# Edge tiles of a dilated attention: two chunks of 128 keys instead of one of 64 and one of 128

## The reference, cut to what matters

```
def dilated_group(q, k, v, dilation, half_steps, bias):
    L = s // dilation                     # tokens of one residue class
    out, lse = banded_attention(to_sub(q), to_sub(k), to_sub(v), half_steps, half_steps, bias, None)

# banded_attention
offs = arange(3 * block)[None, :] - block - arange(block)[:, None]
mask = (abs(offs) <= half_window) & kvalid
logits = where(mask, q @ k * scale + bias, NEG_INF)
e = exp(logits - m);  ssum = sum(e);  out = (e / ssum) @ v
```

## Time and profile before

| | |
|---|---|
| time, median of 3 runs | 2906.52 us (2903.6 to 2906.72) |
| the profiled execution's own time | 2898.05 us |
| its span | 2895.9 us |
| PE busy | 2720.7 us (94%) |
| DVE, ACT, POOL busy | 1310.1 (45%), 1022.5 (35%), 724.5 (25%) us |
| TensorE clock granted, mean | 0.98 |
| branch C in the two layers | from about 707 to 995 us and from 2139 to 2427 us |

### The profile page before, as it was taken

How to read it: one execution, slowest core, us unless ns; L and a number is a source line. 1 busy time by engine, 2 the same in 40 slices (tenths; PEclk the granted TensorE clock), 3 DMA queues, 4 the chain that set the end, 5 groups by cost and what they waited for, 6 DMA issues and landing times.

```text
span 2895.9 us, 36963 instructions
## 1 busy us (share of the span) xinstructions
PE 2720.7 (94%) x13836; PEld 2240.9 (77%) x13836; DVE 1310.1 (45%) x2815; ACT 1022.5 (35%) x2085; POOL 724.5 (25%) x449
## 2 busy tenths in 40 slices
PE   7899999999999989999879999998999999899996
PEld 6677887878888768877776777787888887688875
DVE  3575366522434355523145734585234444455222
ACT  4464116412444425511135631173024443354012
POOL 2100331033434232222220014301333333222231
PEclk9999999999999999999989999999999999999998
DMA  7000210021111221112050011100212113111122
GB/s 241 27 1 10 55 43 19 1 59 45 47 44 41 75 72 30 37 46 95 23 183 15 1 28 46 42 10 10 64 40 52 40 40 103 37 37 37 44 95 80
DMA packets 204194, 146.00 MB, mean 50 GB/s; under 512 B 21688, under 2 KB 187192, under 8 KB 203976
## 3 DMA queue, kind: packets, MB, share of 16 engines
q1 hardware_dynamic: 190188, 137.08, 16.7%
q10 hardware_dynamic: 13824, 6.49, 0.8%
HBM read 124.44 MB, written 27.49 MB: 52 GB/s over the span
## 4 chain that ended last, share of the span: by engine, by line
PE 83%; DVE 9%; ACT 3%; issue 2%; DMA 1%; POOL 1%; SPq 1%; ACTq 0%; POOLq 0%; DVEq 0%; another core or an unknown queue 0%
PE ps L892 21%; PE ps L855 9%; PE ps L856 9%; PE ps L857 9%; PE ps L998 5%; PE ps L1023 4%; PE ps L955 4%; PE ps L956 4%; PE ps L957 4%; PE ps L1071 3%; PE ps L1039 3%; PE ps L1008 2%; DVE pt_slots L1814 2%; PE ps L1000 1%; DVE nm L1650 1%
## 5 line engine op out<-in xcount | busy, mean ns | idle before, releaser
L2051 POOL CAST wh<-wraw 128x1024 fp32r<-128x1024 f32 (+2 forms) x162 | 176.2, 1088 | 2058.8 <-PE ps L857 873.1
L855 PE MATMUL ps<-xh,wh 128*128 128x512 f32 x1120 | 442.1, 395 | 3.0 <-ACT pt_split L1542 2.2
L856 PE MATMUL ps<-xl,wh 128*128 128x512 f32 x1120 | 438.2, 391 | 0.0
L857 PE MATMUL ps<-xh,wl 128*128 128x512 f32 x1120 | 438.1, 391 | 0.0
L2053 POOL TENSOR_TENSOR wl<-wraw,wh 128x1024 fp32r<-128x1024 f32 (+2 forms) x162 | 421.0, 2599 | 13.0
L892 PE MATMUL ps<-xh,wh 128*128 128x512 f32 x864 | 353.9, 410 | 3.1 <-ACT att L1368 1.2
L892 PE MATMUL ps<-xh,wl 128*128 128x512 f32 x864 | 344.4, 399 | 0.0
L892 PE MATMUL ps<-xl,wh 128*128 128x512 f32 x864 | 344.2, 398 | 0.0
L855 PEld LDWEIGHTS ps<-xh,wh 128*128 128x128 f32 x1120 | 212.3, 190 | 47.5 <-ACT pt_split L1542 3.0
L857 PEld LDWEIGHTS ps<-xh,wl 128*128 128x128 f32 x1120 | 211.7, 189 | 44.7
L856 PEld LDWEIGHTS ps<-xl,wh 128*128 128x128 f32 x1120 | 212.1, 189 | 43.2
(11 more groups left out here) (213 smaller groups left out, 4748.1 us busy)
## 6 DMA issues: line engine op xcount, KB each, us to landing
wraw<-in_w_in_dram SPq DMA_DIRECT2D x128, 512.0 KB, 3.9
xres<-acc SPq DMA_DIRECT2D x2, 4096.0 KB, 15.8
toep<-toep_row SPq DMA_DIRECT2D x32, 256.0 KB, 10.7
wraw<-in_w_branch_dram SPq DMA_DIRECT2D x64, 128.0 KB, 3.9
wraw<-in_w_out_dram SPq DMA_DIRECT2D x16, 512.0 KB, 3.7
acc<-xres SPq DMA_DIRECT2D x16, 512.0 KB, 7.7
dil_out<-cst ACTq DMA_DIRECT2D x96, 66.0 KB, 1.6
att<-dil_out SPq DMA_DIRECT2D x48, 132.0 KB, 2.5
```

The costliest lines, as they stand in the source:

```text
L855: pe.matmul(dst, ah, bh, start=i == 0, stop=False)
L856: pe.matmul(dst, ah, bl, start=False, stop=False)
L857: last = pe.matmul(dst, al, bh, start=False, stop=i == len(ks) - 1)
L2051: inc(pool.tensor_copy(high, raw), w_hi)
```

## The change

- The windows of values all have 128 rows. For group 0 they are the seven of the middle and those at 0, 128, 768 and 896 (eleven in all, three groups of transposes of 4, 4 and 3). For group 1 they are those at 0 and 128 of each of the four classes (eight, two groups of 4).
- An edge unit has two chunks of 128 like any other. The first tile of a class takes keys 0 to 255, the last one the last 256; of these the unit sees 192. The probabilities are written at an offset `p0` in `prob`, which is 0 or 64, so that each key stands in its chunk's place; the 64 keys it does not see keep probabilities of zero.
- The zeros are written by a `memset` of 128x64 on DVE ahead of the unit's `maxima`: in group 0 for all four edge units of a pass, in group 1 for the first four units of the first pass only, since later units use the same slot of `prob` with the same part unseen. That is 12 in a layer and 24 in the launch.
- An edge unit's probabilities then come out of PSUM in one copy of 128x256, since both chunks have the same height.
- `at`, where the keys of the logits' product begin, is now the class's own 256 keys for the last tile of a class in group 1. The size of that product, 256 columns, is as before.

```diff
@@ windows and chunks
-                            windows = [(c, P * j - 64, P) for c in range(r) for j in range(1, nq)]
-                            windows += [(c, 0, 64) for c in range(r)] + [(c, L - 64, 64) for c in range(r)]
+                            windows = [(c, P * j - 64, P) for c in range(r) for j in range(1, nq)] if nq > 2 else []
+                            windows += [(c, k0, P) for c in range(r) for k0 in sorted({0, P, L - 2 * P, L - P})]
...
-                                    chunks, at = [], lo
-                                    while at < hi:
-                                        m = 64 if at == 0 or at == L - 64 else P
-                                        chunks.append((m, at - lo, cv[hp][0:m, place[(c, at)], cols]))
-                                        at += m
-                                at = min(k0, S - 2 * P)
+                                    first = min(lo, L - 2 * P)
+                                    at, p0 = c * L + first, lo - first
+                                    chunks = [(P, x, cv[hp][:, place[(c, first + x)], cols]) for x in (0, P)]
+                                    if nk < 2 * P and (nq > 2 or hp == 0 and c == 0):
+                                        fresh = slice(0, p0) if p0 else slice(nk, 2 * P)
@@ exps (ACT)
-                    dst = u["prob"][:, 0:u["nk"]]
+                    p0 = u.get("p0", 0)
+                    dst = u["prob"][:, p0:p0 + u["nk"]]
@@ maxima (DVE)
-                    nk = u["nk"]
-                    ins = dve.tensor_tensor_reduce(u["prob"][:, 0:nk], u["logits"][:, 0:nk], u["bias"], 1.0, 3.0e38,
+                    nk, p0 = u["nk"], u.get("p0", 0)
+                    if u.get("fresh"):
+                        dve.memset(u["prob"][:, u["fresh"]], 0.0)
+                    ins = dve.tensor_tensor_reduce(u["prob"][:, p0:p0 + nk], u["logits"][:, 0:nk], u["bias"], 1.0, 3.0e38,
                                                    ALU.add, ALU.min, mx[:, s % U_MAX:s % U_MAX + 1] if u.get("sink") else dst)
```

More of the change, by code:

```diff
@@ L484, in build @@
                                 cols = slice(e * HD, (e + 1) * HD)
+                                fresh = None
                                 if L == P:
                                     k0, nk, b0 = i * P, P, 0
+                                    at, p0 = min(k0, S - 2 * P), 0
                                     chunks = [(P, 0, cv[hp][:, i, cols])]
@@ L491, in build @@
                                     k0, nk, b0 = c * L + lo, hi - lo, lo - (j * P - 64)
-                                    chunks, at = [], lo
-                                    while at < hi:
-                                        m = 64 if at == 0 or at == L - 64 else P
-                                        chunks.append((m, at - lo, cv[hp][0:m, place[(c, at)], cols]))
-                                        at += m
-                                at = min(k0, S - 2 * P)
+                                    first = min(lo, L - 2 * P)
[3 more added lines that the diff above has]
+                                        fresh = slice(0, p0) if p0 else slice(nk, 2 * P)
                                 unit(cq_stack[hp][:, e, i * P:(i + 1) * P], ck_stack[hp][e][:, 0, at:at + 2 * P],
                                      table_g[:, hp * 2 + e, b0:b0 + nk], chunks, "act",
-                                     st=i, head=hp * 2 + e, e=e, g=g, hp=hp, seen=(k0 - at, nk),
+                                     st=i, head=hp * 2 + e, e=e, g=g, hp=hp, seen=(k0 - at, nk), p0=p0, fresh=fresh,
                                      k_rest=ck_stack[hp][e][:, 1, at:at + 2 * P])
```

## The result

| | before | after |
|---|---|---|
| median of the first runs | 2905.06 us (2901.41 to 2906.72, 4 runs) | 2872.6 us (2869.93 to 2878.59, 4 runs) |
| profiled execution, span | 2895.9 us | 2876.5 us |
| mean granted clock, profiled execution | 0.980 | 0.977 |

The ratio is 0.9893 (0.9873 to 0.9912), 31 us; the two medians are 32.5 us apart. The spans of the two profiled executions are only 19.4 us apart.

What follows compares the result with a forecast made beforehand. PE's own list was taken to bound branch C. 10.8 + 0.3 - 0.2 - 0.6 = 10.3 us a layer, 20.6 in two, off the median 2906.5 gave 2886 us; own spread 2881 to 2891, 8-in-10 range 2878 to 2897.

Steps and rivals of the forecast that it cites:

- PE's own list sets the pace, and the height of 64 rows is what costs: Branch C: PE time saved shortens the kernel; edge units' `values` take 0.62 to 0.64 us against 0.39 because of height.
- The rival that something else in an edge unit costs: Edge units in branch C: the 0.25 us belongs to something that stays; 2906 us, no change, 4% chance.
- 0.278 us for a unit in steady running: Group 1's steady steps: extra cost of an edge unit, 22 units a layer, 6.1 us won.
- 0.26 us for each of the other 18 units of a layer and 0.3 us for the value transposes: Edge units in group 0 or at pass ends: 4.7 us a layer won; value transposes: net 0.3 us a layer.
- Memsets, 0.2 us a layer: DVE in branch C: 4 of 24 memsets exposed, 0.1 us each, costing 0.2 us a layer.
- Given back at the fills, 0.6 us a layer: Group 1's passes: a PE wait at a fill behind DVE's stack work, 2 x 0.3 us a layer lost.
- Sum in branch C: Branch C ends 10.3 us sooner in each layer, 20.6 us in two.
- the change is taken from that median: 2886 us: Whole kernel: the gain is subtracted from the runs' median, 2906.5 us, giving 2886 us, 0.7% faster.
- Slower: Rival at the edge units: wider pieces cost PE weight loads, with all memsets exposed; 8.3 us, 2915 us, 3% chance.
- DVE as pacer: Rival in group 1's passes: DVE's stack work takes back 8 to 16 us, about half the gain; 2896 us, 10% chance.

Runs made afterwards that it cites:

- h64_first: Changed kernel, but the second chunk's value matmul reads 64 rows in the first tile of each class (40 units): 2886.55 us, 0.995 of the kernel before.
- h96_first: Changed kernel, but the second chunk's value matmul reads 96 rows in the first tile of each class (40 units): 2872.62 us, 0.9907 of the kernel before.
- h64_both: Changed kernel, but both value matmuls read 64 rows in the first tile of each class (output wrong): 2887.86 us, 0.9964 of the kernel before.
- h64_last: Changed kernel, but the first chunk's value matmul reads only rows 64 to 127 in the last tile of each class: 2887.84 us, 0.9954 of the kernel before.
- memsets_only: Kernel before plus the 24 memsets of 128x64 in the same places: 2898.83 us, 1.0003 of the kernel before.
- early_rests: Changed kernel with ACT's and DVE's emptying of the next pass's third fill one step earlier: 2874.55 us, 0.9909 of the kernel before.

## Why the prediction was right and wrong, point by point

- **PE's own list sets the pace, and the height of 64 rows is what costs: right.** Shown by h64_first, h96_first, h64_both and h64_last. The rival that something else in an edge unit costs falls. The sentence of the Trainium skill that went with it ("TensorE: Matmul & The Clock Gate", "Why this matters for your kernels": a single matmul with 32 rows takes the same time as one with 128) does not carry over to 64 rows among matmuls of 128: 0.63 against 0.39 us with nothing but the height changed. It may well hold for a matmul alone, which no run here shows.
- **0.278 us for a unit in steady running: right.** The steps came to 3.17 us. With the waits at the fills set aside, the 22 units gave 6.1 us in the first layer.
- **0.26 us for each of the other 18 units of a layer and 0.3 us for the value transposes: together small by 0.3 us a layer.** Forecast were 5.0 us, and the steps of the first layer give 5.3. How this divides is not settled. The step that lost the third group of transposes is 0.68 us shorter; its unit accounts for 0.26 to 0.31 of that, which leaves 0.37 to 0.42 for four transposes instead of 0.35. The two more transposes in the first pass of group 0 took 0.23 us instead of 0.18.
- **Memsets, 0.2 us a layer: nothing** (memsets_only).
- **Given back at the fills, 0.6 us a layer: 0.47** (0.21 + 0.26), and early_rests shows that it is the wait that was named.
- **The first pass of group 2 won 0.26 us that was not forecast.** One step there took 3.33 us with a wait for DVE's copy and now takes 3.07 (942.38 to 945.45). Why DVE is sooner there was not tried.
- **Sum in branch C:** 10.3 us a layer forecast, 11.24 and 11.26 measured. The items above make 0.9 of the difference in the first layer and leave nothing large over. In the launch it is 22.5 instead of 20.6 us.
- **The step that failed is "the change is taken from that median: 2886 us", with the spread given to it.** The median of three runs, 2906.5, lay 7.3 us above the 2899.2 of the 74 later ones. Between 2885.9 (2906.5 less 20.6) and 2872.6 lie 13.3 us: 7.3 are this level, 1.9 are the sum, 3.3 are the first four runs of after against the 17 later ones, and 0.8 are what the pooled medians (23.3) give beyond branch C (22.5). The range gave 3 us to the runs' spread. One kernel's runs spread over 11 to 14 us here, in stretches outside branch C, with the granted clock. The profiled execution of before stood 8.5 us below that median, which was the sign that the level was loose; the sum taken from the profiled execution's own 2898.05 would have given 2877.5, and from 2899.2 it gives 2878.6. That the first four runs of after were low as well, by 3.3 us, is chance as far as the record shows.
- **Slower, and DVE as pacer:** neither came. The steps of group 1 fell to 3.17 us, and of the waits on DVE only the one at the fifth fill is new there.

## What to carry to other kernels

Padding a contraction of 64 rows with zeros up to the height of its neighbours adds no columns and saves the change of height: here 0.26 to 0.30 us for each unit on average, for one cheap memset for each slot, in a stretch where PE's own list sets the pace. Look for such a cost as the distance between starts of the same instructions with and without the odd shape beside them. And read a small gain from the stretch that it touches, by one mark before and one behind it: that repeated to 0.2 us where whole runs spread over 11 to 14.

## What the runs showed of the hardware that was not expected

- 96 rows beside 128 cost nothing, 64 rows beside 128 cost 0.26 to 0.30 us for a visit on average (mostly 0.26 to 0.37 by single steps), whether with two or four instructions in it and whether in rows 0 to 63 or 64 to 127.
- A memset of 128x64 ahead of an addition with minimum on DVE (0.112 us by itself) let the next instruction start 0.02 to 0.03 us later and end after 0.31 to 0.32 us for both, not more than the 0.36 that this took alone. So it was for 22 of the 24 in the changed kernel's trace. The first one of each layer, behind 10.23 us without work on DVE, held the next back by 0.12 to 0.13 us. What makes the difference was not tried.
- The rest of the kernel, outside branch C, took 2324 to 2335 us in 14 traces of kernels that do the same there, with a mean granted clock from 0.976 to 0.982.
